# A two-block layer on one core: the last sum of squares kept on TensorE, two final tiles on GpSimd, two meta columns instead of four, and evacuations and memsets moved

## The chip, the cores and the metric

The kernel runs on one core of one Trainium2 chip. The metric is the device time of one launch, in microseconds (us). Engines: PE is TensorE, ACT ScalarE, DVE VectorE, POOL GpSimd, SP the queue that issues the transfers.

## What is computed

A sequence of 512 tokens of width 1024 goes through two blocks. Nearly all the arithmetic is matrix products with weights that are used once; every norm is an RMS norm over the width.

```python
def rmsnorm(x, g): return x * rsqrt(mean(x * x, -1) + EPS) * g

u = rmsnorm(h, g_mix); z = u @ w_in                 # first block
gq, gk, gv, gr, ga, cx, cb, cc, sq, sk, sv, gates = split_columns(z)   # ga has 16 columns
h = h + merged(gated linear attention, short conv, windowed attention) @ w_o
h = h + (silu(gate) * val) @ w_down                 # gate, val: conv of rmsnorm(h) @ w_up
x = rmsnorm(h, g_final)
h = concat(meta_tokens (16), x)                     # second block: 528 columns
out_a = hgrn2_mixer(...)                            # 8 heads, groups hq hf hi hg
out_b = mamba2_mixer(...)                           # 8 tiles, groups mz mx mb mc dt
h = h + concat(out_a, out_b) @ w_out
h = h + conv_glu_ffn(rmsnorm(h))                    # conv over 3 positions
return rmsnorm(h, final)[:, 16:]
```

The 16 meta columns are dropped at the end. The last convolution reads two positions back, so the first token needs columns 14 and 15 of the layer before it, and no earlier one.

## The kernel before

Activations lie transposed: 128 channels on the partitions, tokens (512, 528, or 516 with four meta columns) along the free axis. Each weight matrix is cut into **units** of 128x128. Eight units are one **slab** of 512 KB, 280 slabs in all. A slab is loaded into `w_raw` by SP, rounded by ACT into `w_hi` (`split_until`), and what the rounding left is written by DVE into `w_lo` (`low_until`, one subtraction of 128x1024). PE does three passes for each unit, `w_hi*u_hi`, `w_lo*u_hi`, `w_hi*u_lo`, in fp32r. A pass over more than 512 columns is two matmuls, cut by `halves`. A **group** is the units that add up to one output tile in PSUM; DVE evacuates it and thereby frees its slot. The first block has 3 slots, the second only 2, so a group's first matmul waits until the group two before it has been evacuated.

Order of work: `schedule()` writes one list, `STEPS`, by hand, and every engine walks through it in that order, doing its own part of each step. A step placed before another on DVE therefore delays it, also where it depends on nothing. The stages around the change:

- **Start.** SP loads gains, slab 0, the eight tiles of x, the rest of the parameters, then slabs 1 and 2. Group `ga` (16 output columns, padded to 8 units, so one slab) comes first, then `gq`, `gk`, `gv`. The norm's root is wanted by all evacuations. Its sum is put on PE ahead of `gk 0` (`SUMS_AT`).
- **First heads of the second block.** Groups `hf h`, `hq h`, `hi h`, `hg h`. DVE's `hf_fin`, `prep_sum` and `prep` make the decayed keys; ACT does tanh, log and exp, with a table load between tanh and log. `second_start` does two things: part 4 clears five buffers (once), and parts 0 to 3 scale the eight tiles of `h_res` that the additions of the groups `oh` need much later. Part 4 and 0 stand behind `hq 0`, 1 behind `hi 0`, 2 behind `hf 1`, 3 behind `hq 1`. `head_a` and `head_b` of head 0 stand behind `hq 1` and `hi 1`.
- **Mamba tiles.** `SSM_ORDER` gives the order of groups, `SSM_PIECES` the work on tile t: a (rows of decays, transposes, products on DVE), b (state), c (output, gate). `sum 0` and `sum 1` make the two group norms, on whose roots (`S["r"]`) the evacuations `om_add` of the groups `om` wait. In `group(g)` DVE does `low_weights(g)` first and then the evacuation. ACT's tanh of `mz 4` and the slab behind it wait until `ssm_sum 0` is done. The evacuation of `om (0, 4)` stands behind `a 7` and `sq 6` ("out 4"). GpSimd does six additions of squares.
- **End.** After `down2 7` DVE adds the residual, ACT squares, DVE adds to the other squares, PE sums over partitions with `ones` (plain fp32), ACT makes the root, DVE scales eight tiles and SP writes each out.

```python
                elif kind == "om" and i != (0, 4):
                    om_add(i)
...
USED = META - 4
```

## Time and profile before

| | us |
|---|---|
| median of three runs (1792.51 to 1793.59) | 1793.43 |
| the profiled execution: its time | 1796.02 |
| the profiled execution: its span | 1794.2 |
| PE busy in the span | 1758.9 (98%) |
| DVE busy | 1175.7 (66%) |
| ACT busy | 717.0 (40%) |
| POOL busy | 10.3 (1%) |

The profiled execution took 1.8 us more than its own span and 2.6 us more than the median. A timeline row gives start, duration, engine, line, operation, output and inputs with their shape, and in brackets the idle time of the engine ahead of it and what ended that. PE's matmuls overlap: their pace is read from the starts, not from the durations. PEclk is the granted clock of TensorE, 1.00 for 2.4 GHz and 0.50 for 1.2 GHz.

### The profile page before, as it was taken

The page shows a single profiled execution, that of the slowest core. Times are in us where ns is not written, and L with a number is a line of the kernel's source. Part 1 is how long each engine was busy: PE and PEld are TensorE (multiplying, and loading weights), DVE is VectorE, ACT ScalarE, POOL GpSimd, SP SyncE. Part 2 cuts the span into 40 slices and gives each one's busy share as a digit, 9 for nine tenths or more (in the row PEclk, how much of TensorE's full clock was granted, in tenths as well). Part 3 has the DMA queues.
Part 4 walks back from the last instruction along what each step waited for, and adds up shares of the span by engine and source line. Part 5 has one row for each costly group of instructions (what it writes and reads, how often), then busy time and mean ns, then how long its engine had stood idle before and what let it go on. Part 6 is the DMA issues. An engine that isn't in the chain of part 4 may idle for free.

```text
span 1794.2 us, 27289 instructions
## 1 busy us (share of the span) xinstructions
PE 1758.9 (98%) x11004; PEld 1535.1 (86%) x11004; DVE 1175.7 (66%) x1811; ACT 717.0 (40%) x1097; POOL 10.3 (1%) x10
## 2 busy tenths in 40 slices
PE   8999999999999999999999999999999999999997
PEld 5778777778878888888889999999988999999885
DVE  5666656656567777734576766788788877777333
ACT  5334433332343333333535454543454433333221
POOL 0000000000000000000000000000000000000000
PEclk9999999999999999999999999999999999999998
DMA  6222222223223233233222122122222232322331
GB/s 198 80 73 83 83 83 76 89 83 94 94 83 95 96 100 93 98 105 95 71 75 75 65 71 71 61 72 72 71 66 68 80 95 95 94 85 94 106 94 59
DMA packets 44540, 154.23 MB, mean 86 GB/s; under 512 B 6000, under 2 KB 6256, under 8 KB 44416
## 3 DMA queue, kind: packets, MB, share of 16 engines
q1 hardware_dynamic: 44416, 152.50, 27.0%
q8 instruction: 87, 1.43, 0.3%
q14 instruction: 37, 0.30, 0.0%
HBM read 150.39 MB, written 2.10 MB: 85 GB/s over the span
## 4 chain that ended last, share of the span: by engine, by line
PE 86%; DVE 8%; ACT 3%; issue 1%; DVEq 1%; ACTq 1%; DMA 0%; SPq 0%
PE ps L619 84%; DVE arena L1294 2%; ACT arena L928 2%; PE ps L623 2%; DVE w_lo L1291 1%; DVEq L1813 1%; DVE arena L1301 1%; ACTq L1274 1%; ACT w_hi L928 1%; DVE u_lo L1493 0%; ACT L933 0%; DVE h_res L1304 0%; DVE h_res L1291 0%; DVE arena L1291 0%; DVE r_bc L1291 0%
## 5 line engine op out<-in xcount | busy, mean ns | idle before, releaser
L619 PE MATMUL ps<-u_hi,w_hi 128*128 128x258 f32 (+3 forms) x2376 | 647.7, 326 | 13.7 <-DVE u_lo L1493 9.0
L619 PE MATMUL ps<-u_hi,w_lo 128*128 128x258 f32 (+3 forms) x2376 | 641.2, 323 | 0.0
L619 PE MATMUL ps<-u_lo,w_hi 128*128 128x258 f32 (+3 forms) x2376 | 639.5, 322 | 0.0
L619 PEld LDWEIGHTS ps<-u_hi,w_hi 128*128 128x128 f32 (+1 forms) x2376 | 395.6, 189 | 58.0 <-issue 14.3
L1291 DVE TENSOR_TENSOR w_lo<-w_raw,w_hi 128x1024 fp32r<-128x1024 f32 x280 | 342.5, 1223 | 152.7 <-ACT w_hi L928 139.9
L619 PEld LDWEIGHTS ps<-u_lo,w_hi 128*128 128x128 f32 (+1 forms) x2376 | 395.0, 189 | 36.9 <-issue 1.4
L619 PEld LDWEIGHTS ps<-u_hi,w_lo 128*128 128x128 f32 (+1 forms) x2376 | 395.0, 188 | 36.6 <-issue 1.6
L928 ACT ACTIVATE w_hi<-w_raw 128x1024 fp32r<-128x1024 f32 x280 | 294.6, 1053 | 313.2 <-PE ps L619 304.5
L1301 DVE SCALAR_TENSOR_TENSOR ffn<-full,par,ffn 128x512 f32<-128x512 f32 (+2 forms) x176 | 132.2, 751 | 81.6 <-ACT ffn L928 78.3
L928 ACT ACTIVATE arena<-arena 128x528 f32<-128x528 f32 (+11 forms) x189 | 96.2, 531 | 212.1 <-DVE arena L1294 91.4
L928 ACT ACTIVATE ffn<-full,par 128x512 f32<-128x512 f32 x88 | 67.8, 771 | 278.2 <-DVE full L1294 278.2
L619 PE MATMUL ps<-a_hi,w_lo 128*128 128x512 f32 x352 | 136.9, 389 | 0.0
L619 PE MATMUL ps<-a_lo,w_hi 128*128 128x512 f32 x352 | 136.9, 389 | 0.0
L619 PE MATMUL ps<-a_hi,w_hi 128*128 128x512 f32 x352 | 136.9, 389 | 0.0
L619 PE MATMUL ps<-arena 128*64 128x128 f32 (+13 forms) x1212 | 117.3, 275 | 5.4 <-ACT arena L928 3.2
L619 PEld LDWEIGHTS ps<-arena 128*64 128x64 f32 (+6 forms) x1212 | 88.5, 150 | 31.7 <-issue 18.2
L1294 DVE TENSOR_TENSOR arena<-arena 128x512 f32<-128x512 f32 (+7 forms) x212 | 79.1, 416 | 15.2 <-ACT arena L928 13.2
L1294 DVE TENSOR_TENSOR full<-ps,r_bc 128x512 f32<-128x512 f32 (+1 forms) x88 | 60.7, 690 | 41.9 <-PE ps L619 40.5
L619 PEld LDWEIGHTS ps<-a_hi,w_hi 128*128 128x128 f32 x352 | 66.1, 188 | 13.8
L619 PEld LDWEIGHTS ps<-a_lo,w_hi 128*128 128x128 f32 x352 | 66.1, 188 | 13.7
L619 PEld LDWEIGHTS ps<-a_hi,w_lo 128*128 128x128 f32 x352 | 66.1, 188 | 13.6
L1294 DVE TENSOR_TENSOR arena<-ps,r_bc 128x516 f32<-128x516 f32 (+3 forms) x68 | 47.4, 696 | 44.0 <-PE ps L619 40.7
(151 smaller groups left out, 1506.8 us busy)
## 6 DMA issues: line engine op xcount, KB each, us to landing
w_raw<-weights SPq DMA_DIRECT2D x280, 512.0 KB, 3.6
h_res<-xT SPq DMA_DIRECT2D x8, 256.0 KB, 5.6
outT<-h_res SPq DMA_DIRECT2D x8, 256.0 KB, 2.1
cst<-consts SPq DMA_DIRECT2D x1, 730.0 KB, 8.5
seg<-consts SPq DMA_DIRECT2D x1, 256.0 KB, 8.6
par<-params SPq DMA_DIRECT2D x1, 240.0 KB, 6.2
...
```

The source lines that it names most:

```text
L619: return nc.tensor.matmul(out, lhsT, rhs, start=start, stop=stop)
L623: return nc.tensor.transpose(out, x, ident[0:k, 0:k])
L928: return nc.scalar.activation(out, in_, func, **k)
L1274: nc.scalar.drain()
L1291: return V.tensor_tensor(out, a, b, op)
L1294: return V.tensor_tensor(out, a, b, ALU.mult)
L1301: return V.scalar_tensor_tensor(out=out, in0=a, scalar=s, in1=b, op0=ALU.mult, op1=ALU.add)
L1813: V.drain()
```

## The change

- `USED` goes from `META - 4` to `META - 2`: groups `hg`, `mz`, `oh`, `om`, `up2` and the norms beside them have 514 columns instead of 516. `halves` now cuts them 258 + 256.
- The `ga` group leaves the unit list (279 slabs). Its weights come as a transfer of their own, 64 KB, first in the queue; x follows, and slab 0 comes behind x. PE does `ga` as 24 matmuls into bank 6. The sum of the first norm moves one group later, to `gv 0`.
- `second_start`: part 4 between `prep_ln` and `prep_sum` of `hf 0`, and parts 0 to 3 at the same place in `hf 1` to `hf 4`.
- Mamba tiles: for `om` groups and `mz 4` DVE evacuates first and does `low_weights` after; `om (0, 4)` is evacuated in its own step, its `low_weights` comes behind `a 7`; ACT does the tanh of `mz 4` and the slab behind it in their ordinary places.
- End: the seven squares are added by DVE as before and summed by PE inside `down2 7` (ahead of its unit 12); the eighth square goes straight to PE, which adds it in PSUM. ACT writes the root to PSUM for DVE and once more to `r_bc` for GpSimd. ACT has multiplied tiles 0 and 1 with their gain into `ffn`, and GpSimd multiplies them by the root. DVE does the other six. The tiles are written out in the order 2, 3, 4, 0, 5, 6, 1, 7.

```diff
@@ -40,12 +40,13 @@
-USED = META - 4
+USED = META - 2
...
+GA = KD * GLA_RANK
...
@@ -68,7 +69,7 @@
-    ("om", (0, 3)): "a 6", ("mx", 7): "b 6; taps mx 7", ("mz", 6): "silu mx 7; c 6", ("om", (0, 4)): "a 7; sq 6; out 4",
+    ("om", (0, 3)): "a 6", ("mx", 7): "b 6; taps mx 7", ("mz", 6): "silu mx 7; c 6", ("om", (0, 4)): "a 7; low; sq 6",
...
@@ -89,7 +90,6 @@
-    full("ga", 0, "w_in", o["ga"])
...
@@ -185,11 +185,12 @@
-    return first if n <= BANK else first + BANK - n // 2
+    return first if n <= BANK else first + BANK - halves(n)[0][1]
...
-    return [(0, n)] if n <= BANK else [(0, n // 2), (n // 2, n)]
+    half = 2 * -(-n // 4)
+    return [(0, n)] if n <= BANK else [(0, half), (half, n)]
...
@@ -227,7 +228,10 @@
-        put("hf", h, ("prep_ln", n), ("slab_behind", GROUP_OF[("hf", h)]), ("prep_sum", n), ("prep_exp", n))
+        put("hf", h, ("prep_ln", n), ("slab_behind", GROUP_OF[("hf", h)]))
+        if h < 5:
+            put("hf", h, ("second_start", (h - 1) % 5))
+        put("hf", h, ("prep_sum", n), ("prep_exp", n))
...
@@ -256,19 +260,19 @@
-    put("hq", 0, ("second_start", 4))
-    for part, where in enumerate((("hq", 0), ("hi", 0), ("hf", 1), ("hq", 1))):
-        put(*where, ("second_start", part))
...
+            if stage == "low":
+                pieces.append(("low", GROUP_OF[where]))
+                continue
...
-                pieces += [("ssm_sum", 0), ("z_tanh", 4), ("slab_behind", GROUP_OF[where])] if n == 4 else []
+                pieces += [("ssm_sum", 0)] if n == 4 else []
...
@@ -282,10 +286,11 @@
-    steps = [("slab", 0)] + [("raw", ("g_mix", k)) for k in range(KD)] + [("slab", 1)]
-    steps += [("square", ("g_mix", k)) for k in range(KD)]
+    steps = [("ga_parts", 0)] + [("raw", ("g_mix", k)) for k in range(KD)] + [("slab", 0)]
+    steps += [("square", ("g_mix", k)) for k in range(4)] + [("slab", 1)]
+    steps += [("square", ("g_mix", k)) for k in range(4, KD)] + [("ga", 0)]
...
-        if GROUPS[g][:2] == ("gk", 0):
+        if GROUPS[g][:2] == ("gv", 0):
...
@@ -297,8 +302,9 @@
-SUMS_AT = {GROUP_OF[("gk", 0)]: ("g_mix", 0), GROUP_OF[("up", (0, 0))]: ("g_ffn", 5),
-           GROUP_OF[("hf", 0)]: ("norm1", 6), GROUP_OF[("up2", (0, 1))]: ("norm2", 0)}
+SUMS_AT = {GROUP_OF[("gv", 0)]: ("g_mix", 0), GROUP_OF[("up", (0, 0))]: ("g_ffn", 5),
+           GROUP_OF[("hf", 0)]: ("norm1", 6), GROUP_OF[("up2", (0, 1))]: ("norm2", 0),
+           GROUP_OF[("down2", KD - 1)]: ("seven", 12)}
...
@@ -574,15 +582,18 @@
+            sp.dma_start(w_raw[:, RAW - 1, 0:GA], w_ga).then_inc(ga_in, 16)
+            for k in range(KD):
+                sp.dma_start(h_res[:, k, META:T2], x_v[:, k, :]).then_inc(x_in[k], 16)
...
+                if s == RAW - 1:
+                    sp.wait_ge(ga_lo_ok, 1)
...
-                    for k in range(KD):
-                        sp.dma_start(h_res[:, k, META:T2], x_v[:, k, :]).then_inc(x_in[k], 16)
...
@@ -591,9 +602,13 @@
-            for k in range(KD):
-                sp.wait_ge(out_ok, k + 1)
-                sp.dma_start(out_v[:, k, :], h_res[:, k, META:T2]).then_inc(out_done, 16)
+            for k in (2, 3, 4, 0, 5, 6, 1, 7):
+                if k < 2:
+                    sp.wait_ge(out2_ok, k + 1)
+                    sp.dma_start(out_v[:, k, :], ffn[:, k, :]).then_inc(out_done, 16)
+                else:
+                    sp.wait_ge(out_ok, k - 1)
+                    sp.dma_start(out_v[:, k, :], h_res[:, k, META:T2]).then_inc(out_done, 16)
...
@@ -608,9 +623,16 @@
+            def last_tiles():
+                pool.wait_ge(final_g, 2)
+                pool.wait_ge(final_r, 1)
+                for k in range(2):
+                    nc.gpsimd.tensor_tensor(ffn[:, k, :], ffn[:, k, :], r_bc[:, 0:SEQ], ALU.mult).then_inc(out2_ok, 1)
...
+            last_tiles()
...
@@ -671,7 +693,29 @@
+            def ga(_):
+                pe.wait_ge(ga_lo_ok, 1)
+                wh, wl = w_hi[:, SPL - 1, :], w_lo[:, SPL - 1, :]
+                for k in range(KD):
+                    hi, lo = u_hi[:, k, META:T2], u_lo[:, k, META:T2]
+                    cols = slice(GLA_RANK * k, GLA_RANK * (k + 1))
+                    pe.wait_ge(u_lo_ok, k + 1)
+                    for j, (wt, x) in enumerate(((wh, hi), (wl, hi), (wh, lo))):
+                        last = mm(ps[0:GLA_RANK, 6, :], wt[:, cols], x, start=(k == 0 and j == 0),
+                                  stop=(k == KD - 1 and j == 2))
+                last.then_inc(ga_end, 1)
+            def seven_squares():
+                pe.wait_ge(sq_added, (KD - 1) * NORMS.index("final") + KD - 2)
+                mm(ps[:, 7, :], ones[:, :], r_bc[:, 0:SEQ], stop=False)
+            def last_square():
+                pe.wait_ge(sq_ok, KD * len(NORMS))
+                mm(ps[:, 7, :], ones[:, :], full[:, (KD - 1) % 2, 0:SEQ], start=False).then_inc(sum_ok, 1)
...
+                if which == "seven":
+                    return seven_squares()
...
@@ -901,13 +945,13 @@
-                mm(ps[:, 6, 384:388], ones[:, :], m_sq[:, g, USED:META]).then_inc(S["sum"], 1)
+                mm(ps[:, 6, 384:386], ones[:, :], m_sq[:, g, USED:META]).then_inc(S["sum"], 1)
...
-                    norm(which)
-            stages = {"norm": last_norm, "group": group, "prep": prep, "head_a": head_a, "head_b": head_b,
+                    last_square()
+            stages = {"norm": last_norm, "ga": ga, "group": group, "prep": prep, "head_a": head_a, "head_b": head_b,
...
@@ -945,11 +989,11 @@
-                if until == 1:
-                    exp_ln()
...
+                    if s == SPL - 1:
+                        act.wait_ge(ga_end, 1)
...
@@ -1007,14 +1051,12 @@
-                elif kind == "mz" and i != 4:
-                    z_tanh(i)
-            def z_tanh(i):
-                if i >= 2:
-                    act.wait_ge(ssm_sem["gated"], i - 1)
-                evacuated(act, GROUP_OF[("mz", i)])
-                f(full[:, i % 2, USED:], m_z[i % 2][:, USED:], ACT.Tanh, scale=0.5).then_inc(act_part, 1)
+                elif kind == "mz":
+                    if i >= 2:
+                        act.wait_ge(ssm_sem["gated"], i - 1)
+                    evacuated(act, g)
+                    f(full[:, i % 2, USED:], m_z[i % 2][:, USED:], ACT.Tanh, scale=0.5).then_inc(act_part, 1)
...
@@ -1027,11 +1069,16 @@
-                if GROUPS[g][0] != "hf" and GROUPS[g][:2] not in (("mz", 4), ("oh", 2)):
+                if GROUPS[g][0] != "hf" and GROUPS[g][:2] != ("oh", 2):
...
+            def ga_parts(_):
+                exp_ln()
+                act.wait_ge(ga_in, 16)
+                f(w_hi[:, SPL - 1, 0:GA], w_raw[:, RAW - 1, 0:GA], ACT.Copy).then_inc(ga_hi_ok, 1)
...
@@ -1064,6 +1111,8 @@
+                if which == "final" and k < 2:
+                    f(ffn[:, k, :], h_res[:, k, META:T2], ACT.Identity, scale=pc("final", k)).then_inc(final_g, 1)
...
@@ -1090,6 +1139,10 @@
+                elif which == "final":
+                    link(f(r_bc[:, 0:n], ps[:, 7, :], ACT.Ln, scale=1.0 / D, bias=pc("eps")))
+                    f(ps[:, 6, :], r_bc[:, 0:n], ACT.Exp, scale=-0.5).then_inc(rstd_ok, 1)
+                    f(r_bc[:, 0:n], r_bc[:, 0:n], ACT.Exp, scale=-0.5).then_inc(final_r, 1)
...
@@ -1318,15 +1371,19 @@
-                if until == 1:
-                    link(V.memset(ones[:, :], 1.0))
-                    V.tensor_copy(ones_r[:, :], ones[:, 0:1]).then_inc(zeroed, 1)
...
+            def ga_parts(_):
+                link(V.memset(ones[:, :], 1.0))
+                V.tensor_copy(ones_r[:, :], ones[:, 0:1]).then_inc(zeroed, 1)
+                dve.wait_ge(ga_hi_ok, 1)
+                tt(w_lo[:, SPL - 1, 0:GA], w_raw[:, RAW - 1, 0:GA], w_hi[:, SPL - 1, 0:GA], ALU.subtract)\
+                    .then_inc(ga_lo_ok, 1)
...
@@ -1357,8 +1414,10 @@
-                low_weights(g)
...
+                late = kind == "om" or (kind, i) == ("mz", 4)
+                if not late:
+                    low_weights(g)
...
@@ -1366,9 +1425,9 @@
-                if kind == "ga":
-                    mul(ga_sb[0:GLA_RANK, :], x[0:GLA_RANK, :], r[0:GLA_RANK, :]).then_inc(free, 1)
-                elif kind == "gq":
+                if g == 0:
+                    mul(ga_sb[0:GLA_RANK, :], ps[0:GLA_RANK, 6, :], r[0:GLA_RANK, :]).then_inc(ga_ok, 1)
+                if kind == "gq":
...
@@ -1429,7 +1488,7 @@
-                elif kind == "om" and i != (0, 4):
+                elif kind == "om":
...
@@ -1454,6 +1513,8 @@
+                if late and (kind, i) != ("om", (0, 4)):
+                    low_weights(g)
...
@@ -1507,7 +1568,7 @@
-                if k:
+                if k and (which, k) != ("final", KD - 1):
...
@@ -1525,8 +1586,8 @@
-                    for k in range(KD):
-                        scaled(h_res[:, k, META:T2], h_res[:, k, META:T2], pc(which, k), r_bc[:, 0:SEQ])\
+                    for k in range(2, KD):
+                        scaled(h_res[:, k, META:T2], h_res[:, k, META:T2], pc(which, k), ps[:, 6, :])\
...
```

## Rows read from the trace of the kernel before

**Rows 1.** The page's first part: busy time of the engines.

```profile
PE 1758.9 (98%) x11004; PEld 1535.1 (86%) x11004; DVE 1175.7 (66%) x1811; ACT 717.0 (40%) x1097; POOL 10.3 (1%) x10
```

**Rows 2.** Who PE waited for: us in total, times, longest.

```profile
PE ps L619 <- DVE u_lo L1493: 9.0, 2, 8.6
PE ps L619 <- DVE h_res L1291: 8.4, 4, 3.5
PE ps L619 <- ACT arena L928: 3.2, 2, 2.6
```

**Rows 3.** Timeline of the start.

```profile
5.23 1.06 ACT L928 ACTIVATE w_hi<-w_raw 128x1024 fp32r<-128x1024 f32 x1 [3.18 <-DMA w_raw<-weights]
...
6.43 6.35 ACT L928 ACTIVATE u_hi<-h_res,par 128x512 fp32r<-128x512 f32 x8
7.71 6.66 DVE L1493 SCALAR_TENSOR_TENSOR u_lo<-h_res,par,u_hi 128x512 fp32r<-128x512 f32 x8 [0.17 <-issue]
...
8.61 0.59 PE L619 MATMUL ps<-u_hi,w_hi 128*16 128x512 f32 x1 [8.61 <-DVE u_lo L1493]
...
16.83 0.39 PE L619 MATMUL ps<-u_hi,w_hi 128*128 128x512 f32 x1
```

**Rows 4.** Timeline of the second block's first heads, DVE and PE.

```profile
891.18 2.19 DVE L1560 MEMSET arena<- 128x2560 f32 x1 [0.66 <-issue]
...
913.97 1.42 DVE L1304 SCALAR_TENSOR_TENSOR h_res<-h_res,par,arena 128x512 f32<-128x512 f32 x2
...
916.60 0.70 DVE L1294 TENSOR_TENSOR arena<-ps,r_bc 128x528 f32<-128x528 f32 x1
...
921.78 1.46 PE L619 MATMUL ps<-arena 16*128 16x128 f32 x6 [2.56 <-ACT arena L928]
```

**Rows 5.** Windows: stretch, us, busy of PE, PEld, DVE, ACT, POOL, PEclk, DMA.

```profile
922.00:924.00 2.00, 2.00 (x11) 1.88 (x11) 0.43 (x2) 0.92 (x1) 0.00 (x0) 0.60 0.64 174
...
1312.00:1314.00 2.00, 2.00 (x11) 2.00 (x11) 1.72 (x6) 0.82 (x6) 0.00 (x0) 0.50 0.17 70
...
1364.00:1366.00 2.00, 2.00 (x9) 2.00 (x10) 1.88 (x3) 0.05 (x1) 0.00 (x0) 0.50 0.00 0
...
1788.00:1789.00 1.00, 0.00 (x0) 0.00 (x0) 1.00 (x3) 0.00 (x0) 0.00 (x0) 0.50 1.03 389
```

**Rows 6.** Timeline around om (0, 0): ACT, DVE, PE.

```profile
1302.07 1.28 ACT L933 ACT_TABLE_LOAD   x1
...
1306.95 0.70 DVE L1308 SCALAR_TENSOR_TENSOR arena<-full,arena 128x516 f32<-128x516 f32 x1 [1.96 <-ACT full L928]
...
1308.47 1.23 DVE L1291 TENSOR_TENSOR w_lo<-w_raw,w_hi 128x1024 fp32r<-128x1024 f32 x1
...
1311.09 0.51 PE L619 MATMUL ps<-u_hi,w_hi 128*128 128x264 f32 x2 [3.52 <-DVE h_res L1291]
```

**Rows 7.** Timeline around om (0, 4) and om (1, 0): DVE and PE.

```profile
1359.88 2.53 DVE L1294 TENSOR_TENSOR arena<-arena 128x512 f32<-128x512 f32 x4 [0.52 <-ACT arena L928]
...
1363.99 0.80 PE L619 MATMUL ps<-v_hi,w_hi 128*128 128x258 f32 x2 [2.69 <-DVE h_res L1291]
...
1381.54 1.23 DVE L1291 TENSOR_TENSOR w_lo<-w_raw,w_hi 128x1024 fp32r<-128x1024 f32 x1 [0.59 <-ACT w_hi L928]
```

**Rows 8.** Groups by form, PE: busy us, mean ns, idle before.

```profile
L619 PE MATMUL ps<-u_hi,w_hi 128*128 128x258 f32 x960 | 195.3, 285 | 1.5 <-DVE h_res L1291 1.1 <-DVE u_lo L1493 0.4
```

**Rows 9.** Timeline of one norm sum inside the stream, and of the end.

```profile
511.07 1.10 PE L619 MATMUL ps<-r_bc,ones 128*128 128x512 f32 x2 [0.46 <-DVE r_bc L1291]
...
1379.11 1.30 POOL L609 TENSOR_TENSOR arena<-arena 128x516 f32<-128x516 f32 x1 [16.72 <-ACT arena L928]
...
1782.02 0.69 DVE L1291 TENSOR_TENSOR r_bc<-r_bc,full 128x512 f32<-128x512 f32 x1 [0.69 <-ACT full L928]
...
1782.86 2.05 PE L619 MATMUL ps<-r_bc,ones 128*128 128x512 f32 x2 [2.26 <-DVE r_bc L1291]
1786.33 5.39 DVE L1304 SCALAR_TENSOR_TENSOR h_res<-h_res,par,r_bc 128x512 f32<-128x512 f32 x8 [3.61 <-ACT r_bc L928]
```

More of the change, by code:

```diff
@@ L503, in program @@
         par_in, cst_in, meta_in, alpha_in = sem("par_in"), sem("cst_in"), sem("meta_in"), sem("alpha_in")
+        ga_in, ga_hi_ok, ga_lo_ok, ga_end, ga_ok = (sem("ga_" + x) for x in ("in", "hi", "lo", "end", "ok"))
         gain_in, x_in = sem("gain_in"), [sem(f"x_in{i}") for i in range(KD)]
@@ L635, in group @@
                     pe.wait_ge(meta_lo_ok, 1)
-                rows = {"ga": GLA_RANK, "dt": M2_R}.get(kind, P)
+                rows = M2_R if kind == "dt" else P
                 out = acc(g, rows)
@@ L692, in prep @@
                     if n == 0:
-                        evacuated(pe, GROUP_OF[("ga", 0)])
+                        pe.wait_ge(ga_ok, 1)
                         pe.wait_ge(alpha_in, 16)
@@ L771, in head_d @@
                 if not gla:
-                    mm(ps[:, 7, 416:420], every, hi[:, 0:m], stop=False)
-                    last = mm(ps[:, 7, 416:420], every, lo[:, 0:m], start=False)
+                    mm(ps[:, 7, 416:418], every, hi[:, 0:m], stop=False)
+                    last = mm(ps[:, 7, 416:418], every, lo[:, 0:m], start=False)
                 last.then_inc(st_d, 1)
@@ L1263, in ssm_sum @@
                 f(r[:, META:T2], ps[:, 5, :], ACT.Ln, scale=1.0 / SEQ, bias=pc("eps"))
[L1264 removed]
+                link(f(r[:, USED:META], ps[:, 6, 384:386], ACT.Ln, scale=1.0 / SEQ, bias=pc("eps")))
                 f(r[:, USED:], r[:, USED:], ACT.Exp, scale=-0.5).then_inc(S["r"], 1)
[L1267 removed]
+            stages = {"ga_parts": ga_parts, "raw": raw, "raw_meta": raw_meta, "slab": lambda s: split_until(s + 1), "square": square, "norm": norm, "bounds": bounds, "group": group_and_slab, "prep": prep, "prep_ln": prep_ln, "prep_exp": prep_exp, "slab_behind": slab_behind, "gate_tanh": gate_tanh, "head_a": head_a, "head_b": head_b, "head_c": head_c,
                       "head_d": head_d, "swa_v": swa_v, "swa_a": swa_a, "swa_b": swa_b, "ssm_dt": ssm_dt,
```

20 lines of the change are left out of this document (9 added, 11 removed).

## The prediction

> **What bounds the kernel now.** I read the busy times first, then what PE waited for, then the timeline around each of its waits, then the granted clock behind them. PE is busy for 98% of the span and its waits are few [rows 1, 2]: the span is PE's stream plus a start, an end and some stalls. So an edit pays where it shortens PE's stream, or where it removes a stall that PE really has. The reader should find four places. At the start PE begins at 8.61 [rows 3]. At 921.78 it has stood 2.56 us for ACT [rows 4]. It stands 3.52 us until 1311.09 [rows 6] and 2.69 us until 1363.99 [rows 7]. The fourth is the end, 13.6 us behind the last product. Each of the three stalls has a second price, which the waits don't list: behind it the granted clock is 0.50 to 0.60 for a stretch [rows 5]. Worked out from the 2 us windows in which it was below 1.00 (two or three for each stall), the work lost is 1.7 us behind the first, 1.7 behind the second, 2.8 behind the third.
>
> **Start.** PE's first matmul needs `u_lo` of tile 0. Before, ACT first rounds slab 0, which has 512 KB to land, and DVE subtracts it, so `u_hi` begins at 6.43 and `u_lo` at 7.71 [rows 3]. Now 64 KB and then x lie ahead. x tile 0 can't land after 5.2, when slab 0 was in with its 512 KB [rows 3], nor before about 4.0, when the 0.33 MB ahead of it would have come at the rate of the windows. I take 4.5. Then `u_hi` 0.73 (a tile of it in the rows of eight is 0.79), `u_lo` 0.76 and PE's 0.14 behind it: first matmul at 6.3, 2.3 us earlier. The 24 small matmuls took 8.2 us before (8.61 to 16.83, [rows 3]) because the first 13 ran at a pace of 0.43 us and the rest at 0.23. `u_lo` comes every 0.83 us for three matmuls and doesn't hold them up. If the fast pace comes at the same moment of the launch instead of equally long after PE's first work, 1 us of the gain goes. Slab 0, now behind 2.1 MB of x, lands at about 10.4 by the rate of the windows (near 400 GB/s); ACT takes it at 10.9, behind the eighth `u_hi`, DVE has it at 13.2. PE asks for it at 14.5, so its cover is 1.3 us. The sum one group later moves the first evacuations to about 29; slot 0 is wanted at 32, so that costs nothing here. I take 2.2 us, range 0.8 to 2.8.
>
> **First heads.** PE waits at 919.2 for ACT's copies, ACT is behind the tanh of `hq 1`, that waits for DVE's evacuation at 916.60 to 917.30 [rows 4], though PE had finished the group at 909.9. DVE was late through the memsets (2.8 us with the small ones, from 891.18) and three pairs of scalings (1.42 to 1.49 us each, the last at 913.97) [rows 4]. Walked through in the new order: the memsets delay `cum_ok` of `hf 0` by 1.9, `hq 0` is evacuated at 892.4 just as PE wants the slot, `hi 0` at 896.8 (0.6 earlier), `prep 0` ends at 905.4 (1.9 earlier), the scalings at `hf 1` lie partly in DVE's 0.98 us wait for ACT's log, and `hq 1` is evacuated at 914.2 instead of 917.3. ACT: table and tanh to 916.2, slab to 917.3, copies to 918.8, ahead of PE's 919.2 by 0.4. The stall and its slow stretch go: 2.6 + 1.7 = 4.3 us. What is late next is PE itself; from `hf 2` on DVE waits 2.57 us for ACT at that place, so parts 1 to 3 are covered. If my walk is late by x, PE loses x over the 0.4. Range 2.5 to 4.4.
>
> **Mamba tiles.** A sum of the stalls would give 3.5 + 1.7 + 2.7 + 2.8 = 10.7 us. I don't take it, because between 1287 and 1371 DVE is idle only in bits of 0.1 to 0.5 us: it binds there as soon as PE is earlier. So I follow DVE. Around `om (0, 0)`: `mz 4` is evacuated at 1302.1, tanh follows at once, and gate 4 no longer waits 1.96 us [rows 6]. But the root now comes behind that tanh, the slab and the table load: 1306.7 instead of 1304.9. The evacuation of `om (0, 0)` runs to 1308.2 (before 1311.04), its `w_lo` [rows 6] to 1309.5. DVE is then 1.8 us earlier than before. PE waits 0.9 for the root ahead of a 5 and 0.3 for the slot. DVE keeps its 1.8 us up to `om (0, 4)`, and PE waits about 1 us each at b 5 and b 6 for the products of a. `om (0, 4)` is now evacuated at 1354.0, before a 7. a 7 still has one 2.53 us piece instead of 1.45 against GpSimd [rows 7]; then two `w_lo` in a row, and `mz 7` is evacuated at 1363.8. PE wants that slot at 1362.4: 1.4 us of waiting in place of 2.69. After b 7 DVE no longer waits 1.79 us for `om (0, 5)`; y 7 comes 4.1 earlier and `om (1, 0)` can be evacuated 4.2 earlier. From there to the last `u_lo` DVE binds. Here the new order has a price: the `w_lo` at 1381.54 lay in a wait for the root [rows 7] and now comes behind the evacuation, on the chain, 1.23 us. Left: 3.0 us. Ends: 1.5 (the 1.8 and nothing later), 6.5 (half of the rest of the stalls too).
>
> **Columns.** 608 units (`oh` 64, `om` 64, `up2` 352, `hg` 64, `mz` 64) x 3 passes = 1824 passes, of which the u-groups have 480 of each kind [rows 8] (two matmuls in each). Two columns at the level 2.4 GHz are 0.83 ns: 1.5 us, all on PE. Slower than that the passes can't become by the weight loads, which are 0.19 us in a pace of 0.24.
>
> **End.** The sum of seven squares joins PE's stream: 511.07 [rows 9] shows such a sum costing 0.93 us until the next product is on pace. +0.9. DVE's addition, 0.69, and its handover go [rows 9]; the sum starts at 1782.14 instead of 1782.86. It took 2.05 us there against 0.93 in the stream, since the clock fell to 0.50 at about 1782.6; 0.7 us earlier, half of its first part may run fast: 0.25, bounds 0 and 0.6. The first scaled tile is then out 0.7 + 0.25 earlier. DVE has six operations of 0.67 instead of eight [rows 9], ending 2.1 us earlier, GpSimd two of 1.3 [rows 9], ending by 1789, beside them. But the transfers set the end: 2.1 MB leave at 389 GB/s with the DMA share at 1.03 [rows 5], for 5.4 us from first to last, so only the earlier first tile counts. Net: -0.95 + 0.9 = about 0; if the queue isn't full after all, 1.3 us more is gained. The trace shows no scaling with its factor in PSUM; evacuations that read PSUM are 0.70, like the others, and one such scaling would have to pass 0.9 to matter.
>
> A row and a rule: against GpSimd, DVE's products took 2.53 instead of 1.45 [rows 7]. The Trainium skill, page "SBUF — State Buffer", section "Who interferes with whom", says that a DVE instruction with two SBUF inputs contends with a GpSimd instruction that reads SBUF, and one with at most one doesn't. By it the final scalings, with the factor in PSUM, are free of this; without it they would end 1 us later, still covered by the transfers. The sum is the same by either.
>
> **Sum.** 2.2 + 4.3 + 3.0 + 1.5 + 0.05 = 11.1 us. Against the span of 1794.2 that is 1783.1. The profiled execution's own time was 1796.02 and the median of the runs 1793.43; a difference carries over, so the median becomes 1782.3. The forecast's own range, with the bounds mostly not at their ends together, is 1779 to 1785.
>
> **The rivals.** (a) *DVE doesn't bind.* If the bits of DVE's idle time add up or PE's waits there are shorter than I walk, the mamba part gives 9.2 (10.7 less the 1.4 at `om (0, 6)`): 6.2 more, 1776. Against it stands DVE's near full occupation. Chance 0.10. (b) *The waits take a slow stretch with them.* PE waits some 10 times for about 1 us in 1305 to 1410. Waits of 1.1 us before had clock 1.00, one of 2.56 hadn't. If several count together, 1.7 to 2.8 us come back: 1784.7. 0.14. The Trainium skill, page "TensorE: Matmul & The Clock Gate", section "What's actually happening", has the throttled clock as the default that activity releases; by that, short waits leave it free, as at 1397 and 1404. (c) *The stall at 919 stays*, since ACT's chain of tables, log and exps binds and not DVE: 4.3 less, 1786.6. 0.08. (d) *Slower:* the second matmul of a pass is now 256 columns wide instead of 258, a width that no fp32r row here has. If below some width such a matmul runs at a lower rate, all 1824 passes pay. The break-even is 11.1 us / 1824 = 6 ns for each pass of 240; at half rate it is 107 ns each, 195 us, 1977. Widths of 258, 264 and 512 all run at a column per clock, so 0.04; it also stands for the case that the edit costs everywhere a little. (e) The forecast: 0.64.
>
> **Range and chances.** 1777.5 to 1786.5: it holds (e), (b) and half of (c), and leaves out (a) in the main, and (d). A measurement tells about 0.2%, 3.6 us, from no change. (e), (a), (b) and (c) are all faster by more than that, but errors of theirs together could reach it: faster 0.91, same 0.04, slower 0.05.
>
> **What would show it.** First matmul near 6.3, first of 128x128 weights near 14.4. No idle time above 0.5 us and clock 1.00 at 915 to 925. Behind `om (0, 1)` waits of about 1 us in place of 3.5 and 2.7, no window under 1.00, DVE without a gap from 1300 to 1405. A pace of 0.2397 in `up2` for 0.2405. At the end DVE done 1.5 us before the transfers' last quarter, at 390 GB/s. A gap over 2 us anywhere in stage two, or slab 0 late at 14.4, makes the prediction wrong.

## The result, and the profile of the changed kernel

The changed kernel takes 1784.65 us (median of 6 runs, 1784.06 to 1785.19), the kernel before 1795.38 (6 runs, 1792.51 to 1797.53): a ratio of 0.9941 [0.9928, 0.9954], 10.7 us faster. The time lies inside the predicted range, 2.35 us above the predicted median. The kernel before spreads widely, and its six runs here lay high: in 28 more, beside the experiments, its median is 1793.57, only 8.9 us above the changed kernel's. The profiled execution took 1784.06 with a span of 1782.3, against 1796.02 and 1794.2: the span is 11.9 us shorter.

The busy times and the list of whom PE waited for, as in [rows 1, 2] (us in total, times, longest):

```profile
PE 1751.8 (98%) x11006; PEld 1527.8 (86%) x11006; DVE 1173.1 (66%) x1808; ACT 717.5 (40%) x1100; POOL 12.3 (1%) x12
...
PE ps L641 <- DVE u_lo L1554: 7.6, 3, 6.3
PE ps L641 <- DVE arena L1347: 5.2, 5, 1.9
PE ps L641 <- DVE h_res L1344: 2.8, 5, 1.2
PE ps L641 <- ACT arena L972: 1.6, 2, 1.0
```

PE is still the bound. Its longest wait outside start and end is 1.9 us; the 3.5 for `h_res` and the 2.6 for ACT are gone. The start, which answers to [rows 3]:

```profile
4.59 1.55 ACT L972 ACTIVATE u_hi<-h_res,par 128x512 fp32r<-128x512 f32 x2 [1.02 <-DMA h_res<-xT]
...
6.32 0.59 PE L641 MATMUL ps<-u_hi,w_hi 128*16 128x512 f32 x1 [6.32 <-DVE u_lo L1554]
...
10.12 0.41 PE L641 MATMUL ps<-u_hi,w_hi 128*16 128x512 f32 x1
...
12.45 1.22 DVE L1344 TENSOR_TENSOR w_lo<-w_raw,w_hi 128x1024 fp32r<-128x1024 f32 x1 [0.19 <-ACT w_hi L972]
...
13.73 0.50 PE L641 MATMUL ps<-u_hi,w_hi 128*128 128x512 f32 x1
```

The first matmul starts 2.29 us earlier, the first 128x128 product 3.10. The slow pace of 0.43 us for a pass held for 9 passes, until 10.12 (before for 14, until 14.52). `w_lo` of the first slab ends at 13.67, only 0.06 before PE uses it.

The first heads of the second block, as [rows 4]: timeline, and the window over the place of the old stall (us, busy PE, PEld, DVE, ACT, POOL, PEclk, DMA share, GB/s):

```profile
883.31 2.19 DVE L1621 MEMSET arena<- 128x2560 f32 x1 [0.66 <-issue]
...
890.11 0.50 PE L641 MATMUL ps<-u_hi,w_hi 128*128 128x258 f32 x2 [0.61 <-DVE arena L1347]
...
907.11 1.42 DVE L1357 SCALAR_TENSOR_TENSOR h_res<-h_res,par,arena 128x512 f32<-128x512 f32 x2
...
911.76 0.70 DVE L1347 TENSOR_TENSOR arena<-ps,r_bc 128x528 f32<-128x528 f32 x1
...
915.00:925.00 10.00, 10.00 (x84) 9.74 (x83) 4.98 (x8) 3.45 (x7) 0.00 (x0) 1.00 0.34 107
```

PE is busy for all of these 10 us at full clock. A new wait of 0.61 stands at 890.11.

Around `om (0, 4)` and `om (1, 0)`, as [rows 7], with the clock's windows, as [rows 5]:

```profile
1351.58 2.56 DVE L1347 TENSOR_TENSOR arena<-arena 128x512 f32<-128x512 f32 x4 [0.27 <-ACT arena L972]
1354.23 2.54 DVE L1344 TENSOR_TENSOR w_lo<-w_raw,w_hi 128x1024 fp32r<-128x1024 f32 x2
...
1357.43 0.51 PE L641 MATMUL ps<-v_hi,w_hi 128*128 128x258 f32 x2 [1.86 <-DVE arena L1347]
...
1373.03 0.69 DVE L1347 TENSOR_TENSOR arena<-ps,arena 128x514 f32<-128x514 f32 x1 [2.39 <-ACT arena L972]
...
1374.37 1.22 DVE L1344 TENSOR_TENSOR w_lo<-w_raw,w_hi 128x1024 fp32r<-128x1024 f32 x1
```

```profile
1358.00:1360.00 2.00, 2.00 (x13) 2.00 (x12) 1.77 (x7) 1.73 (x3) 0.00 (x0) 0.60 0.84 281
1360.00:1362.00 2.00, 2.00 (x11) 1.87 (x9) 1.58 (x3) 0.16 (x1) 0.00 (x0) 0.54 0.12 43
```

At 1357.43 PE has waited 1.86 us for `mz 7`, behind the two `w_lo` in a row. A stretch at half clock follows, 1.7 us of lost work. At 1374.37 is the `w_lo` that now comes behind the evacuation. The end, as [rows 9]:

```profile
1762.36 1.02 PE L641 MATMUL ps<-r_bc,ones 128*128 128x512 f32 x2
...
1771.64 1.13 PE L641 MATMUL ps<-full,ones 128*128 128x512 f32 x2 [1.44 <-ACT full L972]
...
1774.31 4.04 DVE L1357 SCALAR_TENSOR_TENSOR h_res<-h_res,par,ps 128x512 f32<-128x512 f32 x6 [3.37 <-ACT ps L972]
1774.96 2.49 POOL L630 TENSOR_TENSOR ffn<-ffn,r_bc 128x512 f32<-128x512 f32 x2 [404.87 <-ACT r_bc L972]
...
1776.00:1777.00 1.00, 0.00 (x0) 0.00 (x0) 1.00 (x3) 0.00 (x0) 1.00 (x2) 0.50 1.03 383
```

The last sum took 1.13 us where it took 2.05. DVE is done at 1778.35, GpSimd at 1777.45, and the span ends at 1782.3: nothing but transfers runs in the last 3.95 us, and the queue was full before, at 383 GB/s and a share of 1.03.

**The same landmarks in every kernel.** For what follows each trace is cut at five points of PE's stream: the first 128x128 product, the sum of `norm1`, the first group-norm sum (`om (0, x)`), the sum of `norm2`, the last product; then the end of the span. These lengths are differences of start times in the timelines, in us; the tail is what is left to the span, which is given to 0.1, so it is good to 0.05:

```
kernel          start  block 1  heads..  mamba   up2..   tail   span
before          16.83  861.53   420.44   113.02  368.39  13.99  1794.2
changed         13.73  861.60   416.20   111.03  367.25  12.49  1782.3
starts_old      14.14  861.59   421.10   111.03  367.26  12.48  1787.6
mz4_old         14.64  861.49   416.23   112.74  367.27  12.43  1784.8
om04_old        14.41  861.43   416.27   111.97  367.27  12.45  1783.8
four_columns    13.83  861.56   417.10   110.89  369.32  12.40  1785.1
cut_256_258     14.02  861.58   417.62   110.99  370.14  12.45  1786.8
cut_260_256     14.67  861.48   415.79   110.96  366.97  12.43  1782.3
slab_first      15.33  861.60   416.23   111.02  367.26  12.46  1783.9
eight_on_dve    14.18  861.61   416.24   111.01  367.27  12.39  1782.7
root_in_sbuf    14.06  861.60   416.24   111.00  367.27  14.43  1784.6
three_moves     13.97  861.46   415.33   111.52  367.26  12.46  1782.0
all_moves       14.28  861.59   415.01   109.74  367.03  12.45  1780.1
all_moves_warm  14.65  861.61   415.02   111.12  367.02  12.48  1781.9
```

A stretch that an edit doesn't touch agrees within 0.2 us between kernels, so in the table 0.5 us in one stretch can be told, which the time of the whole can't show.

### The profile page after: what moved, and what is told of

Same layout as the page of the kernel before. It is cut to its first block, busy times and chain, and to the rows that moved or that the text cites. A ratio compares the mean times of both kernels' runs of the same rounds, so it can differ in the third digit from the quotient of the medians.

```text
span 1782.3 us, 27294 instructions
## 1 busy us (share of the span) xinstructions
PE 1751.8 (98%) x11006; PEld 1527.8 (86%) x11006; DVE 1173.1 (66%) x1808; ACT 717.5 (40%) x1100; POOL 12.3 (1%) x12
## 4 chain that ended last, share of the span: by engine, by line
PE 85%; DVE 9%; ACT 3%; DVEq 2%; issue 1%; ACTq 1%; DMA 0%; SPq 0%
PE ps L641 83%; DVE arena L1347 2%; ACT arena L972 2%; PE ps L645 2%; DVEq L1874 1%; DVE arena L1354 1%; DVE w_lo L1344 1%; ACTq L1327 1%; DVE h_res L1344 1%; DVE u_lo L1554 0%; ACT w_hi L972 0%; DVE arena L1344 0%; ACT L977 0%; DVE arena L1361 0%; DVE r_bc L1344 0%
## 5 line engine op out<-in xcount | busy, mean ns | idle before, releaser
L1344 DVE TENSOR_TENSOR w_lo<-w_raw,w_hi 128x1024 fp32r<-128x1024 f32 (+1 forms) x280 | 341.5, 1220 | 153.0 <-ACT w_hi L972 141.1
L972 ACT ACTIVATE w_hi<-w_raw 128x1024 fp32r<-128x1024 f32 (+1 forms) x280 | 293.9, 1050 | 302.7 <-PE ps L641 295.9
L1347 DVE TENSOR_TENSOR arena<-ps,r_bc 128x514 f32<-128x514 f32 (+3 forms) x68 | 47.4, 697 | 42.7 <-PE ps L641 36.4
```

What stands on the lines that cost most here:

```text
L972: return nc.scalar.activation(out, in_, func, **k)
L1344: return V.tensor_tensor(out, a, b, op)
L1347: return V.tensor_tensor(out, a, b, ALU.mult)
```

## Experiments

All start from the changed kernel, and none leaves work out. Ratios are against the kernel before.

**starts_old** puts the second block's memsets and scalings back.

```diff
+    put("hq", 0, ("second_start", 4))
+    for part, where in enumerate((("hq", 0), ("hi", 0), ("hf", 1), ("hq", 1))):
+        put(*where, ("second_start", part))
...
-        if h < 5:
-            put("hf", h, ("second_start", (h - 1) % 5))
```

> The changed kernel with the clearing and the scalings of second_start back in their old places (behind hq 0, hi 0, hf 1, hq 1). Forecast: DVE evacuates hq 1 about 3 us later, ACT's copies for head 0 come late, PE waits 2.6 us ahead of head_b 0 near 916, then a stretch at clock 0.5 to 0.6 that costs 1.7; the wait of 0.6 at hg 0 goes. 3.7 us slower than the changed kernel, 1788.3. Rival (ACT's own chain binds, DVE's order doesn't matter): no new wait at 916, 0.6 us faster.

1787.96 us (1785.93 to 1789.35, 7 runs), ratio 0.9960 [0.9946, 0.9975]: 3.3 us slower than the changed kernel, forecast 3.7. In the profiled execution, one of the longest of the seven, the stretch of the heads grows by 4.90, and but for 0.41 at the start nothing else moves. The wait is back at its place, and the new one of 0.61 is gone:

```profile
919.13 2.37 PE L641 MATMUL ps<-arena 16*128 16x128 f32 x8 [2.59 <-ACT arena L972]
...
921.00:923.00 2.00, 2.00 (x11) 2.00 (x10) 1.34 (x4) 0.60 (x1) 0.00 (x0) 0.50 0.44 172
```

So rival (c) falls: DVE's memsets and scalings did make this stall. The same wait that drew 1.7 us of lost work in the trace of before drew 3.4 here (clock 0.50 to 0.52 from 919 to 925, and 0.77 in the 2 us behind).

**mz4_old** sends the tanh of `mz 4` and what follows back to their old places.

```diff
-                pieces += [("ssm_sum", 0)] if n == 4 else []
+                pieces += [("ssm_sum", 0), ("z_tanh", 4), ("slab_behind", GROUP_OF[where])] if n == 4 else []
```

> The changed kernel with only the part around om (0, 0) put back: ACT's tanh of mz 4 and the slab behind it come after the group norm's root, DVE's low_weights of mz 4 and om (0, 0) come ahead of their evacuations. Theory of the prediction (DVE binds from here to the first up2 group): PE's wait at mx 6 is 3.5 us again, but most of it is given back by the waits behind it, so the loss at the start of up2 is 1.8 us, DVE's own delay; 1786.4. Rival (PE binds): 2.3 us more wait and 1.7 us at half clock, 4.0 us slower, 1788.6.

1786.31 us (1785.99 to 1786.68, 5 runs), ratio 0.9956 [0.9938, 0.9974]; the mamba stretch is 1.71 longer.

```profile
1304.64 0.51 PE L641 MATMUL ps<-u_hi,w_hi 128*128 128x264 f32 x2 [3.54 <-DVE h_res L1346]
...
1306.00:1308.00 2.00, 2.00 (x11) 2.00 (x10) 1.77 (x6) 0.83 (x7) 0.00 (x0) 0.50 0.08 31
```

A wait of 3.54 us with 1.7 us of lost clock behind it costs 1.71, the 1.8 by which DVE was forecast to be earlier, and not their sum. The rest is given back: the waits of about 1 us that the changed kernel has behind this place, 0.95 (at 1299.56), 1.01 (1308.11) and 0.98 (1331.90), are gone, and from 1305 to 1359 PE waits nowhere over 0.4. DVE binds, as I had argued.

**om04_old** gives `om (0, 4)` its evacuation behind a 7 again, and no slab weights ahead of the square.

```diff
-    ("om", (0, 4)): "a 7; low; sq 6"
+    ("om", (0, 4)): "a 7; sq 6; out 4"
```

> The changed kernel with only the evacuation of om (0, 4) put back behind a 7 and sq 6, its low_weights ahead of a 7. If DVE binds: the same work in another order, up2 starts within 0.5 us of the changed kernel, though PE's wait before om (0, 5) is near 2.7 us instead of 1.86 and the slow stretch stays; 1784.8. If PE's stall is what counts: 1.0 us of wait more and 1.1 us more at half clock, 1786.7.

1785.71 us (1785.55 to 1786.65, 5 runs), ratio 0.9949 [0.9932, 0.9965]; mamba 0.94 longer, between the theories.

```profile
1356.03 0.51 PE L641 MATMUL ps<-v_hi,w_hi 128*128 128x258 f32 x2 [2.73 <-DVE h_res L1344]
...
1360.72 0.69 DVE L1347 TENSOR_TENSOR arena<-ps,arena 128x514 f32<-128x514 f32 x1 [0.92 <-PE ps L641]
```

Here DVE itself stands 0.92 us for PE, and 0.59 for ACT at 1362.73. "DVE binds" holds up to a 7; behind it DVE and PE wait for each other, and a wait of PE does cost something. Both edits act ahead of the second group-norm sum. There undoing them costs 1.73 (80.34 for 78.61) and 0.95 (79.56), together 2.68 of the 3.05 that the changed kernel gained in that part; behind it both take 32.4, as the changed kernel does. The other 0.37 no run takes apart.

**four_columns** brings back 516 columns, cut 258 + 258.

```diff
-USED = META - 2
+USED = META - 4
```

> The changed kernel with four meta columns again (516, cut 258 + 258). The prediction's price, 0.83 ns for each of 1824 passes: 1.5 us slower, and a pace of 239.2 ns in up2. By the two traces of before and after (240.25 and 238.32 ns a pass, from the starts): 3.5 us slower, pace 240.2. Tells whether the columns alone make the 2.0 us that up2 gained, or something else in the change.

1787.57 us (1786.93 to 1788.33, 6 runs), ratio 0.9964 [0.9949, 0.9980]. Heads +0.90, mamba -0.14, `up2` +2.07: 2.8 us, where I had 1.5. The mamba stretch has a bonus: the wait of 1.82 before `v_hi` is there (the changed kernel's 1.86), but no slow stretch follows at all, and the stretch is nearly as long as with one.

```profile
1358.45 0.51 PE L641 MATMUL ps<-v_hi,w_hi 128*128 128x258 f32 x2 [1.82 <-DVE arena L1347]
...
1369.63 0.51 PE L641 MATMUL ps<-v_hi,w_hi 128*128 128x258 f32 x2 [0.66 <-DVE v_lo L1864]
...
1358.00:1360.00 2.00, 1.55 (x12) 1.56 (x13) 1.80 (x7) 1.38 (x2) 0.00 (x0) 1.00 0.77 287
```

PE, at full clock, then waits 0.66 us for DVE's `v_lo`, where the changed kernel doesn't wait. So the slow stretch at 1358 in the changed kernel costs 0.1 us or little more, not its 1.7: PE has to wait for DVE there anyway.

The pace explains the 2.8: in `up2`, a pass of two matmuls starts every 240.27 ns with four columns (989 passes; before 240.25) and every 238.32 with two (995 passes), 1.95 ns less, where two columns are 0.83. Had all 1824 passes been on the bound, that would be 3.6 us; those of the mamba part gave nothing. Timeline of three passes, before and changed:

```profile
1500.71 0.40 PE L619 MATMUL ps<-u_hi,w_hi 128*128 128x258 f32 x2
1500.95 0.40 PE L619 MATMUL ps<-u_hi,w_lo 128*128 128x258 f32 x2
1501.19 0.41 PE L619 MATMUL ps<-u_lo,w_hi 128*128 128x258 f32 x2
```

```profile
1500.73 0.40 PE L641 MATMUL ps<-u_hi,w_hi 128*128 128x258 f32 x2
1500.96 0.40 PE L641 MATMUL ps<-u_hi,w_lo 128*128 128x258 f32 x2
1501.20 0.40 PE L641 MATMUL ps<-u_lo,w_hi 128*128 128x258 f32 x2
```

What differs beside the number of columns is the column at which the operands start: 12 and 270 before, 14 and 272 now. Two kernels take the number and the second start apart.

**cut_256_258** keeps 514 columns and cuts them 256 + 258, so that the second matmul starts at 270.

```diff
-    half = 2 * -(-n // 4)
+    half = 256 if n == 514 else 2 * -(-n // 4)
```

> The changed kernel, 514 columns, but a pass is cut 256 + 258 instead of 258 + 256: the second matmul reads its operand from column 270 instead of 272. The same columns in all. If the number of columns (or a matmul of 256) makes the pace: 238.3 ns a pass in up2, as in the changed kernel. If it goes by groups of four columns that a matmul touches (14 to 270: 65, 270 to 528: 65, together 130 as with four meta columns, against 129): 240.2 ns, up2 2.0 us longer.

1788.58 us, one run. The pace is 241.12 ns, worse than with 516 columns; heads +1.42, `up2` +2.89. Neither forecast, 238.3 or 240.2 ns, was met.

**cut_260_256** takes four_columns and cuts 516 as 260 + 256, starts 12 and 272.

```diff
-    half = 2 * -(-n // 4)
+    half = 260 if n == 516 else 2 * -(-n // 4)
```

> Four meta columns (516) again, cut 260 + 256 instead of 258 + 258. By the number of columns: 240.2 ns a pass. By groups of four columns touched (12 to 272: 65, 272 to 528: 64, together 129): 238.3 ns, the pace of 514 columns at the price of none fewer.

1784.09 us, one run: 238.05 ns, a little faster than the changed kernel with two columns more. `up2` 366.97. Fewer columns aren't needed for the fast pace; how the second matmul is cut brings it:

```
starts      widths      ns per pass
12, 270     258 + 258   240.25 (before), 240.27 (four_columns)
14, 270     256 + 258   241.12
14, 272     258 + 256   238.32
12, 272     260 + 256   238.05
```

With both starts a multiple of four elements the pass is fastest, with neither slowest. The second start weighs 2.2 to 2.8 ns. The first start and the number of columns always change together, 12 with 516 and 14 with 514: from the first pair to the second the pass gets 0.3 to 0.9 ns longer, so what a first start of 14 costs is more than two columns save, and neither is known alone. The count of groups of four columns gives the order but not the sizes: 130 groups took 240.25 and 241.12, 129 took 238.32 and 238.05. One rival stands: every second piece ends at column 528, so a start at 270 always goes with a width of 258 and a start at 272 with 256. Whether the start or the width of the second piece makes the difference isn't shown, nor whether it is the read of the operand or something tied to it.

**slab_first** sends slab 0 ahead of x, behind the small transfer.

```diff
             for s in range(SLABS):
...
                 if s == 0:
+                    for k in range(KD):
+                        sp.dma_start(h_res[:, k, META:T2], x_v[:, k, :]).then_inc(x_in[k], 16)
```

> The changed kernel with slab 0 issued ahead of the tiles of x, as before the change; the small transfer stays first. Theory: u_hi of tile 0 waits for 0.5 MB more, 1.3 to 1.9 us; PE's first matmul at 7.8 instead of 6.3; slab 0 is ready early, so PE goes on without a wait and the first 128x128 weights start about 1 us later than in the changed kernel, at 14.8 (with 9 slow passes; 0.8 more with 13). Rival: slab 0's w_lo, ready at 13.67 in the changed kernel, bounds the start there (a wait of 0.1), so the order makes less than 0.5 us.

1785.66 us, one run. First matmul at 8.19 (forecast 7.8), first 128x128 product at 15.33 (forecast 14.8):

```profile
8.19 0.58 PE L641 MATMUL ps<-u_hi,w_hi 128*16 128x512 f32 x1 [8.19 <-DVE u_lo L1554]
...
15.33 0.50 PE L641 MATMUL ps<-u_hi,w_hi 128*128 128x512 f32 x1 [0.16 <-DVE w_lo L1344]
```

The order of x and slab gives 1.9 us at the first matmul and 1.6 at the first 128x128 product. The remaining 1.5 of the 3.1 come with the small transfer, and with where in the launch the fast pace begins: this varies, 11.1 here, 10.1 in the changed kernel, 12.1 in cut_260_256, so part of the 1.6 may be its doing as well.

**eight_on_dve** gives the two final tiles back to DVE; the root stays in PSUM.

```diff
-            for k in (2, 3, 4, 0, 5, 6, 1, 7):
+            for k in range(KD):
...
-            last_tiles()
```

> The changed kernel with all eight final tiles scaled by DVE, with the root in PSUM, and none by GpSimd; written out in the order 0 to 7. Theory: the output transfers, full at about 385 GB/s, set the end, so from DVE's first scaling to the end of the span it is 8.0 us as in the changed kernel (8.0) and before (7.9), though DVE ends 1.3 us later. Rival: the two tiles on GpSimd are worth their 1.3 us, 9.3 us.

1784.49 us, one run. From DVE's first scaling (1774.80, eight of 0.67) to the end of the span are 7.9 us, in the changed kernel 8.0, in before 7.9. GpSimd's two tiles bring nothing; the queue sets the end.

**root_in_sbuf** writes the root for DVE into SBUF.

```diff
-                    f(ps[:, 6, :], r_bc[:, 0:n], ACT.Exp, scale=-0.5).then_inc(rstd_ok, 1)
+                    f(full[:, 0, 0:n], r_bc[:, 0:n], ACT.Exp, scale=-0.5).then_inc(rstd_ok, 1)
```

> The changed kernel with DVE's copy of the root in an SBUF buffer of its own instead of PSUM; GpSimd still does two tiles from r_bc. By the contention seen in the mamba part (2.5 us for products that take 1.45 alone): DVE's six scalings take 5.1 to 6.5 us instead of 4.04 and GpSimd's two 1.7 each instead of 1.25. The end moves by less than 0.3 us as long as the transfers set it. Rival (no contention for a product of this form): 4.0 us as before.

1786.40 us, one run. The tail is 1.94 longer, forecast under 0.3:

```profile
1774.69 6.09 DVE L1357 SCALAR_TENSOR_TENSOR h_res<-h_res,par,full 128x512 f32<-128x512 f32 x6 [3.40 <-ACT full L972]
1775.32 2.93 POOL L630 TENSOR_TENSOR ffn<-ffn,r_bc 128x512 f32<-128x512 f32 x2 [404.89 <-ACT r_bc L972]
...
1777.00:1778.00 1.00, 0.00 (x0) 0.00 (x0) 1.00 (x2) 0.00 (x0) 1.00 (x1) 0.50 0.03 10
...
L1357 DVE SCALAR_TENSOR_TENSOR h_res<-h_res,par,full x6: 740/746/1769, 1774.7 to 1780.0; 128x512 f32<-128x512 f32 x6
```

The last row, from the view of this one line of the kernel, gives the shortest, the middle and the longest of the six scalings in ns. They take 1.02 us on the mean instead of 0.67, but not evenly: four last 0.74 to 0.75, as in the changed kernel, and the two that run beside GpSimd's two products 1.77 and 1.75. GpSimd's two take 2.93 instead of 2.49, and in the microsecond after 1777 the queue moves 10 GB/s: it has run dry, and the time is lost. This is what the Trainium skill, page "SBUF — State Buffer", section "Who interferes with whom", says of DVE with two SBUF inputs beside a GpSimd instruction that reads SBUF; the trace agrees (1.77 us beside GpSimd). Before, with both inputs in SBUF too but GpSimd idle, a scaling took 0.67 (5.39 for eight, [rows 9]). The root in PSUM is thus needed only because GpSimd works there, and GpSimd isn't needed.

**three_moves** mends what the trace of the changed kernel shows: `mz 7` is evacuated ahead of the second `w_lo`, the `w_lo` at `om (1, 0)` goes ahead of the evacuation again, and the memsets go back to `hq 0`.

```diff
-                late = kind == "om" or (kind, i) == ("mz", 4)
+                late = (kind == "om" and i != (1, 0)) or (kind, i) in (("mz", 4), ("mz", 7))
...
-        if h < 5:
-            put("hf", h, ("second_start", (h - 1) % 5))
+        if 0 < h < 5:
+            put("hf", h, ("second_start", h - 1))
+    put("hq", 0, ("second_start", 4))
```

> The changed kernel with three steps moved on DVE: the clearing of buffers behind hq 0 again (the scalings stay where the change has them), mz 7 evacuated ahead of its low_weights, and om (1, 0) with its low_weights ahead of the evacuation, inside the wait for the root. Forecast: the wait of 0.61 us at hg 0 goes; PE's wait of 1.86 ahead of om (0, 6) becomes 0.7, which gives nothing by itself where DVE binds; the 1.2 us of w_lo leaves the chain from the root to the last u_lo. 1.8 us faster than the changed kernel. If PE binds in the mamba part: 1.2 us and the slow stretch more, up to 4.5 us faster.

1783.41 us (1783.03 to 1784.51, 4 runs), ratio 0.9938 [0.9919, 0.9957]: 1.2 us faster than the changed kernel, forecast 1.8. The heads gain 0.87, mamba loses 0.49, so the 1.2 us of `w_lo` that were to leave the chain don't show under the slow stretch named next. PE's wait before `v_hi` fell to 0.80, but a wait of 1.84 now stands at 1367.89, and its slow stretch lies on the second group-norm sum, which takes 2.02 instead of 1.24.

**all_moves** adds to it the cut 260 + 256 and moves the low weights behind gate 7.

```diff
+    half = 260 if n == 516 else 2 * -(-n // 4)
...
+                pieces += [("low", GROUP_OF[where])] if n == M2_T - 1 else []
```

> The changed kernel with 516 columns cut 260 + 256, the three moves of three_moves, and the low_weights of om (0, 6) between DVE's gate 7 and v2 7, in DVE's wait of 0.85 for ACT. Forecast against the changed kernel: pace 238.0 in up2, 0.3 us less; 0.9 before the mamba part; gate 7 and with it root and evacuations of om (1, k) 1.2 us earlier, so the stretch from the first group norm's sum to up2 is 110.3 us instead of 111.0. In all 1.9 us faster than the changed kernel. Rival: half clock falls on the new waits and takes 1 us of it.

1782.74 us (1781.89 to 1783.51, 4 runs), ratio 0.9939 [0.9923, 0.9955]: 1.9 us faster than the changed kernel, as forecast. (The ratio is no lower than the changed kernel's 0.9941 because the runs of before beside it have a median of 1792.92, not 1795.38.) In the profiled execution (1781.89) no slow stretch is left between the first product and the last one; heads -1.19, mamba -1.29, `up2` -0.22 against the changed kernel.

**all_moves_warm** lets PE multiply `ones` by itself ten times at the very start, into a bank that isn't in use.

```diff
+                for _ in range(10):
+                    mm(ps[:, 7, 0:P], ones[:, :], ones[:, :])
```

> all_moves with ten fp32 matmuls of ones on ones in PE at the very start, before any data has come, into a bank not yet in use. If PE's own activity ends the slow pace at the start: the 24 matmuls of ga run at 0.23 us from the first on, and the start is bound by slab 0's w_lo: first 128x128 weights at 13.7 in every run (13.7 to 14.7 without). 0 to 1 us faster than all_moves. Rival: the slow pace ends at a moment that doesn't depend on PE: no difference.

1782.53 us (1781.93 to 1783.66, 4 runs), ratio 0.9937 [0.9918, 0.9955]: no difference. The passes run at 0.23 us from 7.54 on, earlier than in any other kernel here (10.0 at the earliest), so PE was at the fast pace early. But then it waits for each `u_lo` (one every 0.84 us) and 0.56 us for `w_lo`, and the first 128x128 product is at 14.65, not at the forecast 13.7 and not earlier than elsewhere (13.7 to 14.7). ACT had waited for tile 2 of x until 7.43 (6.54 in the changed kernel), and so DVE began `w_lo` at 13.37 instead of 12.45. The clock at the start was no longer worth anything.

The two profiled executions differ by 1.4 us in the mamba stretch. That of all_moves_warm has two slow stretches there, that of all_moves none. The first follows a wait of 1.08 us for ACT at 1299.40 (1.04 in all_moves):

```profile
1301.00:1303.00 2.00, 2.00 (x10) 2.00 (x11) 1.74 (x3) 1.90 (x6) 0.00 (x0) 0.52 0.04 14
```

It takes 1.7 us of PE's work, but the part up to the second group-norm sum is only 0.09 us longer (77.93 for 77.84): the wait of 0.98 for DVE that all_moves has at 1307.53 is gone. The second lies on the second group-norm sum; all_moves, then all_moves_warm:

```profile
1368.72 1.24 PE L643 MATMUL ps<-arena,ones 128*128 128x512 f32 x4 [0.16 <-POOL arena L626]
```

```profile
1369.21 2.20 PE L643 MATMUL ps<-arena,ones 128*128 128x512 f32 x4 [0.17 <-POOL arena L626]
...
1369.00:1371.00 2.00, 1.83 (x4) 0.75 (x4) 1.82 (x2) 0.86 (x1) 0.16 (x1) 0.59 0.47 188
```

Both sums follow a wait of 1.3 us for `v_lo`; one execution gets a slow stretch on the sum, the other none, and DVE waits 1.94 us for the root instead of 1.00. From this sum to `up2` are 33.19 us instead of 31.91. Two slow stretches of the same loss, then, cost 0.1 us where PE has to wait for DVE anyway and 1.3 where DVE waits for PE's sum. That fits the runs: all_moves took 1781.9 and 1782.1 at mean clock 0.998, 1783.3 and 1783.5 at 0.996.

## Why the prediction was right, and where it was not

**From the sum to the median: wrong, and as large as the whole miss.** The sum was 11.1 us; the profiled executions differ by 11.9, and 1796.02 - 11.1 = 1784.9 is within 0.3 of the measured median. I took the sum from the median 1793.43 instead, because "a difference carries over". It doesn't when the edit removes the part that varies. The kernel before, in 28 runs beside the experiments, took 1790.6 to 1797.8 us, and with it went the mean granted clock: 1790.6 at 0.997, 1792.4 at 0.996, 1793.8 at 0.994, 1796.0 at 0.992, 1797.6 at 0.991. Its stalls draw slow stretches of unlike length: 1.7 us of lost work at one place in one execution, 3.4 in another kernel's with the same wait. The changed kernel has one, which costs next to nothing; its runs have clock 0.997 or 0.998 and lie within 1.1 us. My sum held 1.7 + 1.7 + 2.8 = 6.2 us of such stretches, near the 5.4 between the profiled execution and the fastest runs of before (1796.02 and 1790.6), so it belonged to that execution. Against the fastest runs of before the change brings some 6 us, against the slowest some 13. None of the fastest runs of before has a trace: that the slow stretches are missing there is read from the mean clock alone.

**Start, 2.2: 3.1 in the trace.** First matmul at 6.32 against a forecast of 6.3. The first fast pass came 4.4 us earlier and not 2.3. Before, the slow passes were 14 and not the 13 that I had read. Over the kernels of this study that keep the order of the transfers the first 128x128 product falls between 13.7 and 14.7, so the forecast of 14.4 is about their middle, and the 3.1 is at the kind end. The cover of slab 0 was 0.06 us, not 1.3: DVE had finished `w_lo` at 13.67 where I had 13.2, and PE wanted it at 13.6 instead of 14.5.

**First heads, 4.3: 3.3.** The heads' stretch got 4.24 shorter, 0.90 of it by the columns. The stall and its slow stretch went, 2.56 + 1.7. The step that failed is the one on `hq 0`: it was to be evacuated "just as PE wants the slot", and PE waited 0.61 for it behind the memsets. three_moves, which undoes that, gained 0.87 there. The 0.3 that is left between 4.26 - 0.61 and 3.3 I have not followed.

**Mamba tiles, 3.0: 2.0.** That the stalls' sum of 10.7 mustn't be taken was right: with the stall of 3.54 and its slow stretch back the stretch is only 1.71 longer. Up to the second group-norm sum the gain was 3.05 (81.66 to 78.61) where I had 4.2; behind it the price of the `w_lo` was 1.06 (31.36 to 32.42), forecast 1.23. The first of these failed: the wait for `mz 7` was 1.86 and not 1.4, and behind a 7 DVE isn't the only bound, as om04_old shows; what makes up the rest of the 1.15 is open. Rival (b), that a slow stretch comes back, is what happened at 1358, but nearly without its price. And short waits did draw one elsewhere: behind 1.04 us in cut_260_256 (clock 0.57 from 1302 to 1306) and 1.08 in all_moves_warm, where I had taken waits of 1.1 as harmless from two of them. Rival (a), 6.2 us more, falls (its 9.2 is 9.3 by its own terms). Of the signs that I had named, the waits of about 1 us came (0.95, 1.01, 0.98), "no window under 1.00" didn't, nor "DVE without a gap": it stood 2.39 us for the root.

**Columns, 1.5: 2.8.** The term had the wrong rate. I priced two columns at 0.83 ns; the pass got 1.95 ns shorter, and cut_260_256 gets that with no column fewer. "All on PE" failed as well: at 1.95 ns the 1824 passes would have given 3.6, but those of the mamba part gave nothing. Rival (d) looked at the width alone too, and the rate did hang on how the cut falls: the other cut of the same 514 columns costs 2.8 ns a pass more. Its "a column per clock" is 215 ns for 516 columns, and the pass took 240.25; there was room for such an effect.

**End, 0.05: 0.6.** The seventh sum costs 0.93 in the stream: `up2` gained 2.07 by the columns, and 1.14 is left. The tail is 1.50 shorter, forecast 0.95: the last sum ran fast throughout (1.13 for 2.05), where I had half of its first part. That GpSimd's tiles bring nothing was right. That without PSUM for the factor the end would still be covered was wrong by 1.9 us (root_in_sbuf).

The terms as measured, 3.1 + 3.3 + 2.1 + 2.8 + 0.6 = 11.9, with mamba at 1.99 plus the 0.14 that the columns took there: two terms too large and three too small nearly cancelled. That is luck: the 0.9 us between forecast and trace hides misses of 0.6 to 1.3 in every term.
